# Expert products of a routed layer: two whole phases with the choice of experts inside them, and gates scattered to DRAM by indirect adding DMAs

## The reference, cut to what matters

```python
def peer_ffn(xn, w_q, sub_keys, expert_u, expert_v):         # t = 512 tokens, d = 1024
    qh = (x2 @ w_q).reshape(t, PEER_HEADS, 2, PEER_QDIM // 2)
    scores = jnp.einsum('thcd,hckd->thck', qh, sub_keys)      # 16 sets of 128 keys
    sv, si = lax.top_k(scores, PEER_TOPK)                     # 16 best of each set
    cand = sv[..., 0, :, None] + sv[..., 1, None, :]
    cv, ci = lax.top_k(cand.reshape(t, PEER_HEADS, 256), PEER_TOPK)
    ...
    experts = (i1 * PEER_NKEYS + i2)                          # 128 of 16384 for each token
    gates = jax.nn.softmax(cv, axis=-1)
    act = jax.nn.gelu(jnp.einsum('tkd,td->tk', expert_u[eb], xb))
    return jnp.einsum('tk,tkd->td', act * gb, expert_v[eb])
...
mod = s_lat @ w_mod[i] + b_mod[i]                             # 1024 x 6144, for two layers
```

## Time and profile before

| | |
|---|---|
| three runs, median | 5555.5 us |
| profiled execution, span | 5551.3 us |
| PE busy | 4686.7 us, 84% |
| DVE busy | 2361.7 us, 43% |
| ACT busy | 1335.0 us, 24% |
| POOL busy | 118.8 us, 2% |
| moved by DMA | 429.83 MB |

### The profile page before, as it was taken

The page is one execution under the profiler, slowest core; times in us unless marked ns, Lnnn a source line. Parts: engine busy times, 40 slices in busy tenths (PEclk is TensorE's granted clock), DMA queues, the critical chain, the costliest instruction groups (busy, mean ns, idle before and its releaser), DMA issues. The chain is left out here.

```text
span 5551.3 us, 65429 instructions
## 1 busy us (share of the span) xinstructions
PE 4686.7 (84%) x23710; PEld 3791.2 (68%) x23710; DVE 2361.7 (43%) x4852; ACT 1335.0 (24%) x2003; POOL 118.8 (2%) x100
## 2 busy tenths in 40 slices
PE   6876886799759999999999596686999979476997
PEld 5765885563547888888888485465888868355776
DVE  2243445349974444444444314454222231454333
ACT  2232222221222222222222222332111122233211
POOL 0000320000000000000000000000000000000000
PEclk9997998899989999999999796787999989588998
DMA  2210002237364333333333110001111111001221
GB/s 94 89 45 25 1 1 72 72 122 238 110 182 145 120 117 125 123 121 117 119 120 105 50 53 1 29 1 45 65 65 57 50 46 46 1 29 47 98 85 67
DMA packets 182330, 429.83 MB, mean 77 GB/s; under 512 B 14512, under 2 KB 81840, under 8 KB 181232
## 3 DMA queue, kind: packets, MB, share of 16 engines
q1 hardware_dynamic: 182128, 427.16, 23.3%
HBM read 391.45 MB, written 35.65 MB: 77 GB/s over the span
## 5 line engine op out<-in xcount | busy, mean ns | idle before, releaser
L276 PE MATMUL psum<-h_hi,w_hi 128*128 128x512 f32 (+1 forms) x1824 | 640.5, 351 | 131.4 <-DVE w_lo L254 131.4
L254 DVE TENSOR_TENSOR w_lo<-w_raw,w_hi 128x1024 fp32r<-128x1024 f32 (+3 forms) x280 | 346.1, 1239 | 905.7 <-ACT w_hi L233 905.0
L277 PE MATMUL psum<-h_lo,w_hi 128*128 128x512 f32 (+1 forms) x1824 | 639.4, 351 | 0.0
L278 PE MATMUL psum<-h_hi,w_lo 128*128 128x512 f32 (+1 forms) x1824 | 638.1, 350 | 0.0
L233 ACT ACTIVATE w_hi<-w_raw 128x1024 fp32r<-128x1024 f32 (+3 forms) x280 | 298.1, 1068 | 762.7 <-PE psum L278 632.8
L276 PEld LDWEIGHTS psum<-h_hi,w_hi 128*128 128x128 f32 x1824 | 350.1, 192 | 179.7 <-DVE w_lo L254 134.5
L1767 PE MATMUL psum<-xn_ffn_hi,ex_w_hi 128*128 128x512 f32 x1024 | 399.5, 390 | 39.0 <-DVE ex_w_lo L1746 39.0
L1715 ACT ACTIVATE ex_w_hi<-ex_raw 128x1024 fp32r<-128x1024 f32 x256 | 270.8, 1058 | 581.8 <-PE psum L1769 544.3
L1768 PE MATMUL psum<-xn_ffn_lo,ex_w_hi 128*128 128x512 f32 x1024 | 399.3, 390 | 0.0
L1769 PE MATMUL psum<-xn_ffn_hi,ex_w_lo 128*128 128x512 f32 x1024 | 399.1, 390 | 0.0
L1767 PE MATMUL psum<-acts_hi,ex_w_hi 128*128 128x512 f32 x1024 | 398.3, 389 | 0.0
(11 more groups left out here) (388 smaller groups left out, 8042.6 us busy)
## 6 DMA issues: line engine op xcount, KB each, us to landing
ex_raw<-in_peer_u SPq DMA_DIRECT2D x128, 512.0 KB, 3.5
ex_raw<-in_peer_v SPq DMA_DIRECT2D x128, 512.0 KB, 3.5
mod_ring<-in_w_mod SPq DMA_DIRECT2D x96, 512.0 KB, 4.4
gates<-gates SPq DMA_DIRECT2D x16, 2048.0 KB, 17.0
gate<-gates SPq DMA_DIRECT2D x128, 256.0 KB, 2.8
w_raw<-in_w_in SPq DMA_DIRECT2D x48, 512.0 KB, 3.5
w_raw<-in_w_gate SPq DMA_DIRECT2D x44, 512.0 KB, 3.5
w_raw<-in_w_up SPq DMA_DIRECT2D x44, 512.0 KB, 3.5
```

What stands on the lines that cost most here:

```text
L254: nc.vector.tensor_tensor(ring.lo[:, j % 2, 0:n], ring.raw[:, j % Ring.SLOTS, 0:n], ring.hi[:, j % 2, 0:n].bitcast(F32), ALU.subtract).the ...
L276: nc.tensor.matmul(o, w_hi, hi, start=(begins and n == 0), stop=False)
L277: nc.tensor.matmul(o, w_hi, lo, start=False, stop=False)
L278: last = nc.tensor.matmul(o, w_lo, hi, start=False, stop=(ends and n == len(terms) - 1))
```

## The change

Stages 2 to 4 become one stage of 256 steps, written out in full with no loops. Each step streams one 512 KB weight tile.

- Steps 0 to 127 (phase U) do all u units. ACT takes gelu of step n-3 before it splits the weights of step n, and SP writes each gelu row (256 KB) to a new DRAM array `gelus`.
- The four blocks of the choice lie in steps 0 to 63. DVE's part is a generator (`choose`) that is advanced by a budget in each step, after the step's subtraction. The scores of the blocks stand on PE ahead of step 0 and behind steps 3, 8 and 24.
- The gates no longer go through one-hot products. DVE works out a cell number for each (token, chosen expert), and POOL adds the gate to that cell of `gates` in DRAM: 512 indirect DMAs of 128 single numbers each. In front of every 16 but a block's first, POOL waits until the earlier ones have landed; two heads may have chosen the same expert.
- `gates` has to be zero before that. POOL clears it inside the product `da_k`, by 64 DMAs of 512 KB from one row of zeros.
- Steps 128 to 255 (phase V) do one row e of experts each: POOL fetches the row of `gates`, SP the row of `gelus`, DVE multiplies, ACT and DVE split, and PE accumulates over all 128 steps in all eight banks. `x` is added once, at the end.
- The modulation leaves PE. Its weights are laid out by output row, 96 pieces of 512 KB, and DVE multiplies and sums 1024 numbers of each partition (two conditions for the first 64 pieces, one for the others) in steps 66 to 248.
- There are three slots for the split weights in place of two.

```diff
-                     act=lambda t, s, b: nc.scalar.activation(kk[:, t, :], ps[:, b, :], ACT.Copy))
+                     act=lambda t, s, b: nc.scalar.activation(kk[:, t, :], ps[:, b, :], ACT.Copy),
+                     pool=k.clear_gates)
...
+        if pool:
+            @block.gpsimd
+            def _(eng):
+                pool(eng)
...
+            def mod_tiles_by(n):
+
+                if n < MOD_AT:
+                    return 0
+                return min(MOD_TILES, -(-MOD_TILES * (n - MOD_AT + 1) // (2 * P - 8 - MOD_AT)))
...
+                for n in range(2 * P + RAW):
+                    if n < 2 * P:
+                        if n >= RAW:
+                            sp.wait_ge(low, n - RAW + 1)
+                        src = io["peer_u"][n, :, :] if n < P else io["peer_v"][n - P, :, :]
+                        sp.dma_start(raw[:, n % RAW, :], src).then_inc(w_in[n % RAW], 16)
+                    if 7 <= n < P + 7:
+                        put_gelu(n - 7)
+                    if 0 <= n - P - 1 < P:
+                        get_gelu(n - P - 1)
+                    if n == MOD_AT - 6:
+                        sp.wait_ge(scored, TB)
+                        sp.dma_start(cond[:, :, :], io["c_rows"].broadcast_to([P, 2, D]))\
+                            .then_inc(cond_in, 16)
+                    for tile in range(mod_tiles_by(n - 1), mod_tiles_by(n)):
+                        get_mod(tile)
...
+            def _(pool):
+                cells = io["gates"].rearrange("a b t -> (a b t)").unsqueeze(1)
+                pool.wait_ge(k.zeroed, 16 * k.zeroing)
+                for t in range(TB):
+                    pool.wait_ge(chosen, t + 1)
+                    for h in range(PEER_HEADS):
+                        if h:
+
+                            pool.wait_ge(landed, 16 * (t * HT + h * NK))
+                        for j in range(h * NK, (h + 1) * NK):
+                            nc.gpsimd.indirect_dma_start(
+                                cells, bass.IndirectOffsetOnAxis(ap=cell[:, t, j:j + 1], axis=0),
+                                gate[:, t, j:j + 1], None, compute_op=ALU.add)\
+                                .then_inc(landed, 16)
+                pool.wait_ge(landed, 16 * TB * HT)
+                for e in range(P):
+                    s = e % RAW
+                    if e < RAW:
+                        pool.wait_ge(peaked, TB)
+                    else:
+                        pool.wait_ge(weighted, e - RAW + 1)
+                    pool.dma_start(gate_in[:, s, :], io["gates"][e, :, :]).then_inc(gate_at[s], 16)
...
+                pe.wait_ge(keys_in, 16)
+                scores(0)
+                for n in range(P):
+                    if n >= U_BANKS:
+                        pe.wait_ge(gelued, n - U_BANKS + 1)
+                    pe.wait_ge(low, n + 1)
...
+                        nc.tensor.matmul(o, a, xn[0][:, t, :], start=(t == 0), stop=False)
+                        nc.tensor.matmul(o, a, xn[1][:, t, :], start=False, stop=False)
+                        last = nc.tensor.matmul(o, b, xn[0][:, t, :], start=False,
+                                                stop=(t == KD - 1))
+                    last.then_inc(used, 1)
+                    if n == 3:
+                        scores(1)
+                    if n in (8, 8 + STEP):
+                        scores(2 + n // STEP)
+                for e in range(P):
+                    n = P + e
+                    pe.wait_ge(low, n + 1)
+                    pe.wait_ge(weighted, e + 1)
+                    hi, lo = (weighted_parts[:, i, e % PARTS, :] for i in range(2))
+                    for t, bank in enumerate(V_BANKS):
+                        if e == 0 and t == 0:
+                            pe.wait_ge(kept, TB)
+                        if e == 0 and bank == 0:
+                            pe.wait_ge(gelued, P)
+                        a = w_hi[:, n % PARTS, bank * P:(bank + 1) * P]
+                        b = w_lo[:, n % PARTS, bank * P:(bank + 1) * P]
+                        nc.tensor.matmul(ps[:, bank, :], a, hi, start=(e == 0), stop=False)
+                        nc.tensor.matmul(ps[:, bank, :], a, lo, start=False, stop=False)
+                        last = nc.tensor.matmul(ps[:, bank, :], b, hi, start=False,
+                                                stop=(e == P - 1))
+                        if e == P - 1:
+                            last.then_inc(summed, 1)
+                    if e < P - 1:
+                        last.then_inc(used, 1)
...
+                keep_scores(0)
+                for n in range(2 * P):
+                    if n >= PARTS:
+                        act.wait_ge(used, n - PARTS + 1)
+                        if n - PARTS < P:
+                            m = n - PARTS
+                            if m >= RAW:
+                                act.wait_ge(stored[m % RAW], 16 * (m // RAW))
+                            nc.scalar.activation(gel[:, m % RAW, :], ps[:, m % U_BANKS, :],
+                                                 ACT.Gelu_apprx_tanh).then_inc(gelued, 1)
+                    act.wait_ge(w_in[n % RAW], 16 * (n // RAW + 1))
+                    nc.scalar.activation(w_hi[:, n % PARTS, :], raw[:, n % RAW, :], ACT.Copy)\
+                        .then_inc(high, 1)
+                    if n >= P:
+                        e = n - P
+                        act.wait_ge(made, e + 1)
+                        nc.scalar.activation(weighted_parts[:, 0, e % PARTS, :],
+                                             gate_in[:, e % RAW, :], ACT.Copy).then_inc(act_high, 1)
...
+                def modulate(tile):
+                    s = tile % MOD_RING
+                    dve.wait_ge(mod_in[s], 16 * (tile // MOD_RING + 1))
+                    both = tile < MOD_TILES // LAYERS + 2 * KD
+                    if both:
+                        wait_from(dve, mod_used, tile)
+                        V.scalar_tensor_tensor(product, mod_w[:, s, :], 1.0, cond[:, 1, :],
+                                               ALU.mult, ALU.mult, accum_out=mods[:, tile, 1:2])
+                    last = V.scalar_tensor_tensor(mod_w[:, s, :], mod_w[:, s, :], 1.0, cond[:, 0, :],
+                                                  ALU.mult, ALU.mult, accum_out=mods[:, tile, 0:1])
+                    last.then_inc(mod_used, 1)
...
+                choosing, spent = iter(()), 0.0
+                for n in range(2 * P):
+                    dve.wait_ge(high, n + 1)
+                    V.tensor_tensor(w_lo[:, n % PARTS, :], raw[:, n % RAW, :],
+                                    w_hi[:, n % PARTS, :].bitcast(F32), ALU.subtract)\
+                        .then_inc(low, 1)
+                    if n % STEP == 0 and n // STEP < TB:
+                        choosing, spent = choose(n // STEP), 0.0
+                    while spent < 3.5 * (n % STEP + 1):
+                        spent += next(choosing, 1000.0)
+                    if P - 1 <= n < 2 * P - 1:
+                        make(n - P + 1)
+                    if n >= P:
+                        e = n - P
+                        dve.wait_ge(act_high, e + 1)
+                        V.tensor_tensor(weighted_parts[:, 1, e % PARTS, :], gate_in[:, e % RAW, :],
+                                        weighted_parts[:, 0, e % PARTS, :].bitcast(F32),
+                                        ALU.subtract).then_inc(weighted, 1)
+                    if n == MOD_AT + 2:
+                        dve.wait_ge(cond_ready, 1)
+                    for tile in range(mod_tiles_by(n - 2), mod_tiles_by(n - 1)):
...
+        def clear_gates(pool):
+            nc.gpsimd.memset(mods[:, :, :], 0.0)
+            nc.gpsimd.memset(zeros, 0.0).then_inc(zero_made, 1)
+            pool.wait_ge(zero_made, 1)
+            for e in range(0, P, ZERO):
+                pool.dma_start(io["gates"][e:e + ZERO, :, :].rearrange("a b t -> b a t"),
+                               zeros.unsqueeze(1).broadcast_to([P, ZERO, T]))\
+                    .then_inc(k.zeroed, 16)
```

More of the change, by code:

```diff
@@ L1361, in experts @@
-def experts(k, io, x, xn, modulation):
+MOD_TILES = LAYERS * 6 * KD
+def experts(k, io, x, xn, mods, b_mod):
     nc, ps = k.nc, k.ps
@@ new lines, in experts @@
+        qk = sb("peer_qk", [P, (SETS + 4) * T])
+        qh = qk[:, 0:SETS * T].rearrange("p (s n) -> p s n", n=T)
+        keys = qk[:, SETS * T:(SETS + 4) * T].rearrange("p (s n) -> p s n", n=P)
+        with weight_ring(k) as ring:
+            gemm(k, "peer_q", ring, [io["w_peer"]], 1, [[(0, T, terms_of(xn, KD), True, True)]],
+                 act=lambda t, s, b: nc.scalar.activation(qh[:, t, :], ps[:, b, :], ACT.Copy))
+        MOD_RING = 4
+        mod_w = qk[:, 0:MOD_RING * D].rearrange("p (s n) -> p s n", n=D)
@@ new lines, in experts @@
+        part = sb("part", [P, 2, PEER_HEADS, NK], U32)
+        partf = sb("partf", [P, 2, PEER_HEADS, NK])
+        picked = sb("picked", [P, 2, HT])
+        total = sb("total", [P, PEER_HEADS])
```

(20 more changed lines are left out.)

618 lines of the change are left out of this document (184 added, 434 removed).

## The result

The changed kernel takes 5616.0 us (median of 4 runs, 5610.8 to 5618.1) against 5556.1 for the kernel before beside it: the ratio is 1.0105, 95% interval 1.0091 to 1.0120. It is slower by 1%, where 5131 us was forecast. Its profiled execution has a span of 5608.7 us, 482 more than the sum of the prediction (5126.7).

A forecast was written before the change was run, and what follows sets the result against it. DVE was taken to bound 430 us, a store 39 and PE 1394, one behind the other. 5551.3 - 461.0 (earlier products) + 16.4 (scores) + 20 (clearing) = 5126.7, plus 4.2 for the median: 5131 us, range 5095 to 5400.

The forecast's parts named there:

- The scatters: POOL's 512 indirect DMAs during U: taken 1.05 us each, bounds 0.33 and 2.8, through 30 us before U ends.
- the other estimate: A scatter's price by packets: 8 on each of 16 DMA engines at 0.114 us each, so 0.9 us.
- scatters late: Rival: V waits for POOL from 1.11 us a scatter; at 1.5 us, 5332 us. Chance 0.33 (below 1.94 us each).
- slower: Rival: each scatter costs a whole trip, eating the gain from 1.94 us on; 5946 us at 2.8. Chance 0.09.
- The page's rule: Fixed 2.0 us per scatter, mostly waiting for completion: 5536 us if each in turn, little change if overlapping.
- POOL beside DVE: POOL and DVE disturb each other: DVE 1.75 us beside POOL (median 0.75), POOL 1.65 against 1.26 alone.
- The start of the products: PE's step 0 starts at about 1211.8 in place of 1672.8, 461.0 us earlier.
- The clearing: 64 DMAs of 512 KB in POOL's queue inside da_k: bounds 0 and 100 us, taken 20.
- PE's pace: U and V keep 128 times 24 matmuls each, at 5.445 us a unit of 24: no change.
- the rival's 83 us: Rival: the clearing holds da_k, 83 us beyond the stage and a few in dv, near 5200 us. Chance 0.04.
- DVE and DMA keep up: In the steps DVE needs 4.48 of 5.445 us, DMAs 243 GB/s in V; no loss taken.
- The sum: Against the profiled execution: 5551.3 - 461.0 + 16.4 + 20 = 5126.7 us.

The follow-up runs named there:

- e_half: Changed kernel with only every second gate scattered (256 of the 512 adding DMAs; output lacks half the gates): 5175.0 us, ratio 0.931 to the kernel before.
- e_moved: Changed kernel with the clearing of the gates issued by POOL during the dilated attention stage instead of da_k: 5578.0 us (10 runs).
- v_low: Changed kernel with two blocks scattered under U, two made by one-hot products, clearing in attention, raw and split weights allocated first: 5249.9 us, ratio 0.944.
- b_top: Kernel before with raw and split weights both at the top of its buffers, at the changed kernel's addresses: 5599.3 us, ratio 1.0083.
- b_shift: Kernel before with 32 bytes put in ahead of its raw weights, all buffers still low: 5581.0 us.
- b_shift64: Kernel before with 64 bytes put in ahead of its raw weights, all buffers still low: 5580.2 us.
- e_align128: Changed kernel with the small buffer total at 128 bytes a partition instead of 32, so split weights start at 0 modulo 128: 5600.5 us.
- e_both128: Changed kernel with the clearing issued during attention and the buffer total at 128 bytes a partition: 5555.2 us (12 runs), ratio 1.0010 to the kernel before.
- e_plain: Changed kernel with scatters that write instead of adding (output lacks gates where an index occurs twice): 5508.2 us, one execution.

## Why the prediction was wrong

The mechanism on which all hung was named (V can't start before the last scatter has landed, break-even 1.11 us), and the size put into it, the price of one scatter, was wrong. Term by term, against the profiled execution:

- **The scatters (taken 1.05 us each, none late).** This term failed. A scatter costs 1.631 + 0.322 = 1.953 us, and 512 times the difference of 0.90 us is 462 of the 478 us that POOL took longer. The landing waits make the rest, 68 us for 52. The price was borrowed from POOL's computing row of 1.04 us. That row shows arithmetic on 128 partitions, and nothing of issuing a DMA of 128 numbers with an add; the DMA engines' packets, the other estimate (0.9 us), were no limit either: in the hole they stood at a share of 0.22. The bounds, 0.33 and 2.8, held the value, and its neighbour, a landing of 1.8, would have been nearer. What came has the mechanism of the rival "scatters late" (0.33): they are issued one behind the other, and landings are waited for only between groups of 16. Its size lies just above that rival's span, in the one from 1.94 us on that "slower" had (0.09). At 1.95 us the rival's sum gives 512 x 1.95 + 52 - 619 = 431 us, the hole that came. That it fits so well is luck: U ended 645 us after the first scatter and not 625, and the landing waits took 16 us more, which cancels. The range stopped at 1.63 us.
- **The page's rule.** By the Trainium skill, DMA: Bandwidth & Descriptors, Anatomy of one DMA — SWDGE (gpsimd) path, the sum was 5536 us, with 2.0 us for each scatter. The measured 1.95 us agrees in size. The trace shows another cause than a wait for completion, though: 1.55 to 1.63 us of it is time in which POOL is busy, and only 28 landings between groups are waited for. That the sizes agree may be chance, since without the add one is busy 0.96 us.
- **POOL beside DVE.** The prediction feared a mutual hold. Something of the kind is there and small: a scatter's mean is 1.74 us in e_half, where all lie beside busy engines, and its median 1.55; in the changed kernel's hole none is over 1.57. Over 512 scatters, (1.631 - 1.552) x 512 = 40 us. Whether DVE is what holds POOL, or the DMAs beside it, no run separates.
- **The start of the products (1211.8).** Right: 1206.3 and 1209.5 where the clearing is out of the way (e_moved, v_low).
- **The clearing (taken 20, bounds 0 and 100).** 38 us by e_moved. The fork was seen rightly: POOL could issue its last DMAs only as fast as data went, and the barrier waited. The price in it was worked out with 258 GB/s; da_k moved 390 GB/s, so the rival's 83 us became 38, under half. dv's share of it is the later start, not slow loads.
- **PE's pace (taken unchanged).** This failed too, for a cause that no step of the prediction looked at: what the change did to buffer addresses. It is 41 us over both phases, of which only V's 21 count here, since U's fall into the hole. In the kernel before, b_top shows the size, and b_shift and b_shift64 that it is the weights' place relative to the moving data. For the changed kernel itself this is likely and not shown (e_align128, e_both128).
- **DVE and DMA keep up.** Right. U has PE busy 355.8 of 360 us with DVE at 283.6; V moved 243 GB/s with PE full, the rate that was worked out.
- **The sum.** The first product came 13 us later than with the 20 of the sum; from there to V's first product were 1160 us for 713, and V took 718 us for 697; behind V, 1 us. That makes the 482.
- **Chances.** "Slower" got 0.09, decided from 1.94 us a scatter with the rest as forecast. The costs that come on top when V waits for the scatters, 18 us more for the clearing, 21 for V's pace and 16 for the landings, lower that point to 1.83 us: (1.94 x 512 - 55) / 512. The rival was priced as if it had to beat the whole forecast alone.

## What to carry to other kernels

What 512 DMAs of single numbers cost here was the time that the issuing engine spent on them, so count instructions times the time of one, and measure one before 512 of them are put on a path; hide as many as fit under other work (here 256) and make the rest in another way. When costs could each come out high, price the losing case with all of them at once. Where transfers are put into an earlier stage, its barrier waits until the last of them is issued; here 4 of 64 DMAs that could not be issued in time cost nearly all of the 38 us. When buffers are moved, look at the duration of a matmul in the middle of a full stretch: 7 ns of 389 are 41 us over 6144 matmuls.

## What the runs showed of the hardware

- An adding indirect DMA with 128 numbers keeps POOL busy 1.55 us, with 64 numbers 1.42, without the add 0.96, and 0.3 us lie between two of them (medians).
- POOL issued 60 DMAs of 512 KB at 0.72 us each, and then none for 55 us while the DMA engines moved 372 GB/s (180 to 200 us).
- In the one execution with plain scatters of single numbers, loads, stores and PE's issue (one matmul in 2.8 us) came almost to a stop for some 350 us. Before and after it the same scatters ran beside a full PE, so they are not shown to be the cause.
- A 128x128x512 matmul of this kernel repeats every 226.7 ns or every 233.3 ns. In the kernel before it was the slow one where weights and moving data start at different bytes modulo 128. In the changed kernel, with both at 0 and the weights high, the traces show medians of 393 to 398 ns.
- The Trainium skill, SBUF — State Buffer, Who interferes with whom, says that PE never waits on anyone. No run here tests it between engines. b_top shows that PE's pace can still change by addresses alone, by 7 ns a matmul; and what held PE in e_plain isn't known.
